# Transposes of values and b ahead of the gram products in a head pair's opening

## The reference, cut to what matters

```
def step(S, inp):
    r_t, d_t, k_t, v_t, a_t, b_t = inp
    sa = jnp.einsum('bhij,bhj->bhi', S, a_t)
    S = (S * d_t[:, :, None, :] + sa[..., None] * b_t[:, :, None, :]
         + v_t[..., None] * k_t[:, :, None, :])
    return S, jnp.einsum('bhij,bhj->bhi', S, r_t)

_, y = lax.scan(step, state0, tuple(seq_first(z) for z in (r_h, decay, k_h, v_h, vec_a, vec_b)))
```

## Time and profile before

| what | us |
|---|---|
| median of 3 runs | 2482.78 |
| lowest and highest of them | 2482.14, 2487.97 |
| the profiled execution, its whole time | 2482.47 |
| the profiled execution, its span | 2480.5 |

### The profile page before, as it was taken

One profiled execution on the slowest core, in us unless ns is written; L12 is line 12 of the kernel. 1 busy time (PEld: TensorE's weight loads), 2 busy tenths in 40 slices (PEclk: granted clock), 3 DMA queues, 4 the chain that ended last, 5 costly groups with the idle time before them and its releaser, 6 DMA issues.

```text
span 2480.5 us, 33541 instructions
## 1 busy us (share of the span) xinstructions
PE 2371.9 (96%) x13710; PEld 1195.7 (48%) x13710; DVE 895.6 (36%) x2187; ACT 572.9 (23%) x1211; POOL 0.2 (0%) x4
## 2 busy tenths in 40 slices
PE   7999999988999999989978999999899998999998
PEld 3555555564444444454434444444444655444553
DVE  6455555541522220034405222210236266131542
ACT  2222222212211110035513111100221253113550
POOL 0000000000000000000000000000000000000000
PEclk9999999979999999999989999999999998999998
DMA  3100000002212121111162212221112110111011
GB/s 113 47 31 31 31 31 31 19 19 104 84 68 85 68 97 70 70 43 43 43 124 102 85 69 83 70 91 70 57 68 83 54 35 35 68 68 63 31 43 68
DMA packets 25264, 154.56 MB, mean 62 GB/s; under 512 B 2476, under 2 KB 2604, under 8 KB 11308
## 3 DMA queue, kind: packets, MB, share of 16 engines
q1 hardware_dynamic: 22032, 145.57, 16.4%
q10 hardware_dynamic: 3100, 7.08, 1.6%
HBM read 146.61 MB, written 6.03 MB: 62 GB/s over the span
## 4 chain that ended last, share of the span: by engine, by line
PE 91%; DVE 5%; DMA 2%; issue 1%; ACT 1%; SPq 0%; DVEq 0%; ACTq 0%
PE banks L1384 23%; PE banks L1146 12%; PE banks L1057 8%; PE banks L1086 7%; PE banks L1744 4%; PE banks L470 3%; PE banks L438 3%; PE banks L1596 2%; PE banks L460 2%; PE banks L1630 2%; PE banks L1608 2%; PE banks L2328 2%; DMA arena<-o_attn 2%; PE banks L575 2%; PE banks L1399 1%
## 5 line engine op out<-in xcount | busy, mean ns | idle before, releaser
L1384 PE MATMUL banks<-arena 128*128 128x512 f32 x1344 | 577.7, 592 | 0.0
L1384 PEld LDWEIGHTS banks<-arena 128*128 128x128 f32 x1344 | 255.0, 190 | 319.6 <-issue 318.7
L1146 PE MATMUL banks<-arena 128*128 128x512 f32 x704 | 303.0, 591 | 0.0
L1439 DVE SCALAR_TENSOR_TENSOR arena<-banks,arena 128x511 f32<-128x511 f32 (+1 forms) x176 | 132.0, 750 | 387.4 <-ACT arena L1422 375.3
L1057 PE MATMUL banks<-arena 128*128 128x512 f32 x512 | 227.8, 606 | 14.6 <-DMA arena<-o_attn 14.6
L1146 PEld LDWEIGHTS banks<-arena 128*128 128x128 f32 x704 | 133.0, 189 | 169.7 <-issue 169.7
L1316 DVE TENSOR_TENSOR arena<-arena 128x512 f32<-128x512 f32 x70 | 48.3, 690 | 408.7 <-ACT arena L1275 405.2
L1422 ACT ACTIVATE arena<-banks,arena 128x512 f32<-128x512 f32 x88 | 68.1, 778 | 474.7 <-PE banks L1384 460.3
L1086 PE MATMUL banks<-arena 128*128 128x512 f32 x384 | 168.3, 595 | 0.0
L1057 PEld LDWEIGHTS banks<-arena 128*128 128x128 f32 x512 | 98.9, 195 | 141.1 <-issue 124.3
L1744 PE MATMUL banks<-arena 128*128 128x512 f32 x256 | 124.6, 614 | 0.0
(11 more groups left out here) (280 smaller groups left out, 2607.2 us busy)
## 6 DMA issues: line engine op xcount, KB each, us to landing
arena<-up SPq DMA_DIRECT2D x44, 1024.0 KB, 4.8
arena<-down SPq DMA_DIRECT2D x16, 1408.0 KB, 6.0
arena<-w_mix SPq DMA_DIRECT2D x8, 1728.0 KB, 7.4
arena<-e_in SPq DMA_DIRECT2D x12, 1024.0 KB, 4.8
arena<-o_in SPq DMA_DIRECT2D x8, 1024.0 KB, 4.8
arena<-w_o SPq DMA_DIRECT2D x4, 1024.0 KB, 4.8
arena<-q SPq DMA_DIRECT2D x8, 512.0 KB, 3.3
arena<-o_attn SPq DMA_DIRECT2D x4, 1024.0 KB, 14.8
```

Source lines behind the costliest of these rows:

```text
L1146: ins = pe.matmul(k.ps[:, j, :], k.ring[s][:, t * P:t * P + P], source[:, t, :], start=t == 0, stop=t == FT - 1)
L1384: ins = pe.matmul(k.ps[:, UP + 2 * s + m, :], k.ring[s][:, (m * KT + t) * P:(m * KT + t + 1) * P], source[:, t, :], start=t == 0, stop=t = ...
L1439: dve.scalar_tensor_tensor(conv[j][:, shift:T], k.ps[:, UP + j, 0:T - shift], k.vec("conv", col + tap), conv[j][:, shift:T], ALU.mult, ALU ...
```

## The change

In `opening_tensor` the transposes of V and B move from behind the grams to between low and the grams. The wait for y_square of the pair before, which guards bank 7, goes with them; the wait for G on ScalarE now stands ahead of the transposes and the grams. The transposes of K stay behind the grams. No operation is added or removed, and nothing changes on the other engines' lists.

```diff
         S.done(ins, "low")
         pe.wait_ge(A.sem, A.at(n, "g"))
+        if n:
+            pe.wait_ge(self.tail_act.sem, self.tail_act.at(n - 1, "y_square"))
+        self.turned_tensor(pe, n, ("V", "B"))
         for i in range(2):
             for c in range(4 * i, 4 * i + 4):
                 cols = slice(c % 4 * P, c % 4 * P + P)
@@
                 for rows, other in self.PLACES:
                     ins = pe.matmul(ps[other, 4 + i, cols], kc[rows, c, :], ar[rows, c, :], start=True, stop=True)
             S.done(ins, f"gram{i}")
-        if n:
-            pe.wait_ge(self.tail_act.sem, self.tail_act.at(n - 1, "y_square"))
-        self.turned_tensor(pe, n, ("V", "B"))
         pe.wait_ge(V.sem, V.at(n, "bonus"))
         self.turned_tensor(pe, n, ("K",))
```

## The result

| | before | changed |
|---|---|---|
| median of 10 runs, us | 2483.24 | 2490.93 |
| lowest and highest, us | 2482.14, 2490.74 | 2488.69, 2494.86 |
| profiled execution: time, span, us | 2482.47, 2480.5 | 2494.14, 2492.2 |

The account below looks back on a forecast made before the run. TensorE, 96% busy, was taken as the bound, with VectorE the tight neighbour. 7 x 0.60 = 4.2 us plus 0.75 for pair 7 made 4.95; on 2482.47, plus 0.31 for the median, 2487.7 us, range 2484.0 to 2490.2.

Parts of the forecast that it names:

- The wait ahead of the dense steps: Pairs 0 to 6: late gram_k0 on VectorE delays TensorE's dense steps, a gap of some 0.5 to 0.8 us before L438.
- I take 0.60: Delay in us chosen for the dense steps in each of pairs 0 to 6, together 4.2 us.
- The bounds of 0.54 and 0.78: Lowest and highest worked-out delay in us of the dense steps per pair, the highest with a costlier stalled start.
- Pair 7: No dense steps; gram_b1's shift on VectorE, 0.73 us or 0.84 by the other bound, reaches the end; taken as 0.75.
- a clock below 1.00 ahead of the scan: Sign against the forecast: TensorE's granted clock below 1.00 (2.4 GHz) before pair 7's scan.
- The rival: Slower by more, 9%: pair 7's stall makes TensorE's clock fall early, at 509, costing 8.0 us extra, 2495.7 us.
- The sum: Pairs 0 to 6 at 0.60 us each, 4.2 us, plus 0.75 for pair 7: 4.95 us slower.
- likeliest case: Loss as worked out, 2.5 to 6.3 us more, so 2485.3 to 2489.1 us; chance 75%.
- The moved wait for y_square: TensorE's opening: costs nothing, since y_square ends at 137.72 and low's last products start at 138.02, cover 0.3 us.
- One reason that the prediction gives: V and B transposes have their inputs by then, since low and the grams read the same arrays.
- V beside low: Size inside the main case: V's transposes run beside low, gaining at most 0.25 us; total loss 2.5 us, 2485.3 us.
- The earlier copies on ScalarE: V's and B's copies can start some 1.8 us sooner but gain nothing, since K's copy still waits for K's transposes.

Follow-up runs that it names:

- e1: Changed kernel with the order of before restored in pair 7, so the new order in pairs 0 to 6 only; ratio 1.0015, median 2488.04 against 2483.77.
- e3: Changed kernel with gram_k0 put ahead of gram_b1 on VectorE; ratio 0.9999, median 2483.49 against 2483.77 us for the kernel before.
- e4: Changed kernel with K's transposes also moved ahead of the grams; ratio 1.0053, median 2498.27 against 2483.77 us for the kernel before.
- e6: Kernel before, V transposes alternating with low's products and K's with B's on idle tiles, y and y_square ahead of G; ratio 1.0010, median 2485.40 against 2482.71.
- e2: Changed kernel with the new order kept in pair 7 only; ratio 0.9996, median 2484.32 against 2483.77 us for the kernel before.
- e7: e6 with gram_k0 put ahead of gram_b1 on VectorE; ratio 0.9993, median 2481.30 against 2482.71 us for the kernel before.
- e9: e7 with K's products ahead of B's in each chunk but the last; ratio 0.9980, median 2479.79 against 2484.22 us for the kernel before.
- e11: e9 and e10 together; ratio 0.9981, median 2479.69 against 2484.31 us for the kernel before.
- e5: Kernel before with gram_k0 put ahead of gram_b1 on VectorE; ratio 1.0004, fastest run 2481.72 against 2481.72 us.
- e10: e7 with TensorE's opening of before kept in pair 7; ratio 0.9975, median 2478.62 against 2484.22 us for the kernel before.

## Why the prediction was right in kind and small in size

- **The wait ahead of the dense steps.** Shown: predicted in pairs 0 to 6 and ended by VectorE's L868; there are seven such waits in the changed kernel, e1 carries 4.3 us of the loss by itself, e3 removes it with the wait alone, and e4 doubles the gap with the delay.
- **Its size.** The step "I take 0.60" was mis-sized: the pairs stand 61.36 us apart instead of 60.68, so a pair loses 0.68. Two parts make it up. The shift of gram_b1 against low was 0.79 us (142.01 - 138.08 = 3.93, against 140.23 - 137.09 = 3.14) and not 0.73, since V with B and the grams took longer in the chain than the 0.91 and what the grams took before: the last two L547 alone stand there with 0.16 us, where the last two grams had 0.04. Why was not shown. And TensorE started 0.14 us after gram_k0's end (143.30 to 143.44), not 0.05. Together 0.54 + 0.06 + 0.09 = 0.69. The bounds of 0.54 and 0.78 held it.
- **Pair 7.** The shift of the VectorE chain was 0.81 us (low to T copy 7.90 instead of 7.09), inside 0.73 to 0.84. What was not in the sum is the clock: pair 7 lost 1.30 us in the profile, so 0.5 goes with the clock, with its short fall from 516.6 to 520.0. The prediction had named a clock below 1.00 ahead of the scan as a sign that it was wrong, and this sign is there in the first profile. The rival named this mechanism and priced it for a fall through all the levels (8 us); in fact it fell for a short time, and it was given 9% as an all-or-nothing case instead of a term of 0.3 to 1.1 us in the sum.
- **The sum.** 7 x 0.68 + 1.3 = 6.1 us for the change itself, with the profile's 4.66 for the seven pairs 6.0, against 6.55 by the fastest runs, 6.7 by the ratio and 7.7 by the medians. What makes up the rest is not shown. The forecast's likeliest case ended at 2489.1, and the 2489.5 that the ratio gives lies within the range only by the 1 us that it kept for the clock.
- **The moved wait for y_square** cost nothing, as said. The V transposes started at 138.85, under the last products of low, with no gap. One reason that the prediction gives is not right: low and the grams read B but not the values, which only their transposes read. What covers V's input is the wait for G, ahead of which ScalarE copies the values.
- **V beside low.** The step that V could gain up to 0.25 us there did not come about: V's first passes went ahead of low's last ones (L520 at 138.85), as L544's did in the earlier trace rows, but the grams came no earlier for it. e6 shows the tiles do run side by side when the products alternate in the program.
- **The earlier copies on ScalarE** brought nothing, as e3 shows: V and B were copied early in it, and its time is that of before.

Left open: what decides whether the clock falls in pair 7's levels. It fell in the profiles of the changed kernel, e2, e4, e6, e7, e9 and e11, and not in those of before, e1, e3, e5, e10 and the second run of the changed kernel. Neither the opening, nor the time of pair 7's start, nor a fall in pair 0 sorts these.

## What to carry to other kernels

Work of equal length on a full engine can be reordered for free only as far as its readers have slack: here a 0.91 us move met 0.24 us of slack, and the difference was paid in each pair. Look for what waits on the buffer's release as well as on the data: the products that were late were not needed by the dense steps at all, only their bank was, and reading that bank first (gram_k0 ahead of gram_b1) made the new order free. The same reading first is what turns TensorE's shorter opening in e6 into time in e7, e9, e10 and e11.

## What the runs showed that was not expected

- Matmuls on different 64x64 tiles ran side by side only where they alternate in the program. V behind low overlapped it for the last few passes (138.85 to about 139.03), and not for want of y_square: in pair 0, where V waits for none, it began 0.76 us after low (78.98 against 78.22), and in pair 1 0.77; alternating, low with V took 0.98 us from its first product to the first L542 (196.54 to 197.52 in e7, where that is L556), exactly what low takes alone (258.73 to 259.71 before).
- TensorE's start after VectorE's end was 0.05 us in one place and 0.14 in another, the second for a product that waits on several semaphores, as does the dense step. That the number of semaphores is the reason was not tried, though the 0.14 is what the sum lacked.
- The clock fell from 516.6 to 520.0 in a stretch where TensorE was busy 4.50 of 5.00 us, and in the kernel before stayed up with 4.62 of 5.00; the 11 us ahead of that differed little too (9.54 us busy against 9.88).
